# Differential attention: scores of both halves in three banks, the second softmax joined by a ratio, the division applied at the output

## What is computed

```
s = einsum("bhiqd,bhikd->bhiqk", q, k) * 64 ** -0.5      # i = 0, 1: the two half heads
p = softmax(s, axis=-1)
a = p[:, :, 0] - lam * p[:, :, 1]
o = einsum("bhqk,bhkd->bhqd", a, v)
out_da = merge_heads(rmsnorm(o, da_subln) * (1.0 - lambda_init))
```

## Time and profile before

| | us |
|---|---|
| median of 3 runs | 1944.46 (1941.73 to 1947.86) |
| the profiled execution | 1941.84 |
| its span | 1940.0 |
| PE busy in the span | 1747.5 (90%) |
| DVE busy | 756.4 (39%) |
| ACT busy | 514.0 (26%) |
| mean granted clock of PE | 0.952 |

### The profile page before, as it was taken

How to read it: one execution, slowest core, us unless ns; L and a number is a source line. 1 busy time by engine, 2 the same in 40 slices (tenths; PEclk the granted TensorE clock), 3 DMA queues, 4 the chain that set the end, 5 groups by cost and what they waited for, 6 DMA issues and landing times. The chain is left out here.

```text
span 1940.0 us, 26208 instructions
## 1 busy us (share of the span) xinstructions
PE 1747.5 (90%) x11374; PEld 1242.3 (64%) x11374; DVE 756.4 (39%) x1086; ACT 514.0 (26%) x899; POOL 138.3 (7%) x113
## 2 busy tenths in 40 slices
PE   3889999977894999999999799988895899999997
PEld 1678876656653444344443588877895478888886
DVE  2522224777434122222222577515547233333332
ACT  2311224821231110111111433233343222323231
POOL 0100000000000000000000022104411010101010
PEclk9899998988996999999999899988988999999999
DMA  9112112035323999999999523100000333322201
GB/s 365 48 44 87 44 44 87 1 139 211 128 105 123 426 430 430 430 430 429 430 429 426 215 89 113 61 1 1 5 4 1 141 141 105 111 89 87 87 1 44
DMA packets 60171, 319.19 MB, mean 165 GB/s; under 512 B 5437, under 2 KB 5773, under 8 KB 45465
## 3 DMA queue, kind: packets, MB, share of 16 engines
q1 hardware_dynamic: 60056, 317.51, 40.9%
HBM read 313.31 MB, written 4.19 MB: 164 GB/s over the span
## 5 line engine op out<-in xcount | busy, mean ns | idle before, releaser
L1508 PE MATMUL bank<-ring,xinT 128*64 128x512 f32 x592 | 131.5, 594 | 1.7 <-ACT slot_affinity L1581 1.7
L590 DVE TENSOR_TENSOR in_w_lo<-ring,in_w_hi 128x1024 fp32r<-128x1024 f32 x32 | 41.9, 1310 | 175.6 <-ACT in_w_hi L557 175.6
L250 PE MATMUL bank<-h4T_hi,mlp_w_hi 128*128 128x512 f32 (+1 forms) x288 | 105.8, 367 | 0.3 <-PEq L2460 0.3
L2635 DVE TENSOR_TENSOR mlp_w_lo<-ring,mlp_w_hi 128x1024 fp32r<-128x1024 f32 x60 | 74.0, 1234 | 80.8 <-ACT mlp_w_hi L2594 80.8
L250 PE MATMUL bank<-h4T_lo,mlp_w_hi 128*128 128x512 f32 (+1 forms) x288 | 105.2, 365 | 0.0
L250 PE MATMUL bank<-h4T_hi,mlp_w_lo 128*128 128x512 f32 (+1 forms) x288 | 105.2, 365 | 0.0
L250 PE MATMUL bank<-mlp_w_hi,up_hi 128*128 128x512 f32 x256 | 100.0, 391 | 3.5 <-DVE x L2647 3.5
L250 PE MATMUL bank<-hT_hi,in_w_hi 128*128 128x512 f32 (+1 forms) x256 | 94.6, 370 | 8.5 <-DVE hT_lo L621 4.9
L250 PE MATMUL bank<-mlp_w_hi,up_lo 128*128 128x512 f32 x256 | 99.7, 389 | 0.0
L250 PE MATMUL bank<-mlp_w_lo,up_hi 128*128 128x512 f32 x256 | 99.6, 389 | 0.0
L1508 PE MATMUL bank<-expert_slab,xinT 128*64 128x512 f32 x432 | 95.9, 594 | 0.0
(11 more groups left out here) (437 smaller groups left out, 3730.6 us busy)
## 6 DMA issues: line engine op xcount, KB each, us to landing
ring<-w_gate SPq DMA_DIRECT2D x19, 2048.0 KB, 20.9
ring<-w_up SPq DMA_DIRECT2D x18, 2048.0 KB, 20.8
ring<-w_down SPq DMA_DIRECT2D x17, 2048.0 KB, 19.7
ring<-mlp_w SPq DMA_DIRECT2D x16, 2048.0 KB, 8.5
expert_slab<-w_down SPq DMA_DIRECT2D x15, 2048.0 KB, 21.1
expert_slab<-w_up SPq DMA_DIRECT2D x14, 2048.0 KB, 19.9
expert_slab<-w_gate SPq DMA_DIRECT2D x13, 2048.0 KB, 17.3
ring<-w_ada SPq DMA_DIRECT2D x12, 2048.0 KB, 9.3
```

Of the source, the lines that this page charges most:

```text
L250: mm = pe.matmul(out, x, y, start=(start and i == 0), stop=(stop and i == 2))
L590: dve.tensor_tensor(lo, slab_part(m, s, i, by_rows), hi, ALU.subtract).then_inc(w_lo, 1)
L1508: mm = pe.matmul(bank[half * H:(half + 1) * H, b, :], xin[:, 4 * r + k, (e % 2) * H:(e % 2 + 1) * H], expert_slab(m, s)[:, k, half * COLS: ...
L2635: dve.tensor_tensor(lo, slab_part(m, s, i, n is not None), hi, ALU.subtract).then_inc(w_lo, 1)
```

## The change

- Scores of unit n lie in three banks (0 to 2 or 3 to 5, by the unit's parity), both halves side by side: 1536 columns. The matmuls have 512, 256, 512 and 256 columns, for halves 0, 1, 1, 0. Both halves touch the middle bank, so the last matmul waits on a new semaphore for the first one of half 1. One semaphore tells that both halves are there.
- Scores of unit m wait for the exps of unit m-2 and no longer for those of m-1.
- The second softmax is no longer scaled by ACT. DVE forms ratio = -lam * sum0 / sum1 and the difference is exps1 * ratio + exps0. 1/sum0 is applied as the scale of the output copy.
- Transposes go to banks 6 and 7, three blocks of 128 columns in each, and ACT copies them in two parts. The product with v goes to the columns of bank 6 that the transposes leave free; there is one such place, so product n-2 also waits for the first part of the turned difference n-1.
- The orders: PE transposes n-1, scores n+1, product n-2. DVE both reductions of n+1, then reciprocal, ratio and difference of n. ACT exp (n, first), the two copies of n-1, exp (n, second), the piece of `m.kl`, output copy n-2.
- The squares for `da_ss` move to `recurrence`, where ACT makes them from `mix_da` behind its first copy.

```diff
-            for n in range(-1, N + 2):
...
-                        if n >= 0:
-                            pe.wait_ge(exp_ready, 2 * n + 1 + i)
...
+            def turn(w):
+                pe.wait_ge(diff_ready, w + 1)
+                if w >= 2:
+                    pe.wait_ge(pv_out, w - 1)
+                for j in range(AT):
+                    mm = pe.transpose(bank[:, 6 + j // 3, (j % 3) * P:(j % 3 + 1) * P], a[:, w % 2, j * P:(j + 1) * P], m.ident)
+                    if j % 3 == 2:
+                        mm.then_inc(turned, 1)
+            def score(n):
+                h, t = units[n]
+                if n >= 2:
+                    pe.wait_ge(exp_ready, 2 * (n - 1))
+                for i, c0, c1 in ((0, 0, COLS), (1, 0, TA - COLS), (1, TA - COLS, TA), (0, COLS, TA)):
+                    r = slice(HD * i, HD * (i + 1))
+                    if (i, c0) == (0, COLS):
+                        pe.wait_ge(shared_scored, n + 1)
+                    mm = pe.matmul(scores(n, i)[:, c0:c1], q[r, h, t * P:(t + 1) * P], k[r, h, c0:c1], start=True, stop=True)
+                    if (i, c0) == (1, 0):
+                        mm.then_inc(shared_scored, 1)
+                mm.then_inc(scores_ready, 1)
+            def apply(w):
+                h = units[w][0]
+                pe.wait_ge(diffT_ready, 2 * w + 2)
+                if w + 1 < N:
+                    pe.wait_ge(diffT_ready, 2 * (w + 1) + 1)
+                else:
+                    pe.wait_ge(pv_out, w)
...
+            score(0)
+            for n in range(N + 2):
+                if 1 <= n <= N:
+                    turn(n - 1)
+                if n + 1 < N:
+                    score(n + 1)
+                if n >= 2:
+                    apply(n - 2)
...
+            for n in range(N + 2):
+                if n < N:
+                    exp_of(n, 0)
+                if 1 <= n <= N:
+                    w = n - 1
+                    for i in range(2):
+                        act.wait_ge(turned, 2 * w + i + 1)
+                        act.activation(aT[:, w % 2, i * THIRD:(i + 1) * THIRD], bank[:, 6 + i, 0:THIRD], ACT.Copy).then_inc(diffT_ready, 1)
+                if n < N:
+                    exp_of(n, 1)
...
+                    act.activation(out[:, t, h * P:(h + 1) * P], pv, ACT.Copy, scale=ri[:, w, 0:1]).then_inc(pv_out, 1)
...
+            def difference(n):
+                dve.wait_ge(exp_ready, 2 * n + 2)
+                dve.reciprocal(ri[:, n, :], rs[:, n, :]).then_inc(inv_ready, 1)
+                dve.wait_ge(inv_ready, 2 * n + 1)
+                dve.scalar_tensor_tensor(out=ratio[:, n, 0:1], in0=rs[:, n, 0:1], scalar=ri[:, n, 1:2], in1=m.neg_lam[:, :],
+                                         op0=ALU.mult, op1=ALU.mult).then_inc(inv_ready, 1)
...
+                dve.scalar_tensor_tensor(out=a[:, n % 2, :], in0=e[:, n % 2, 1, :], scalar=ratio[:, n, 0:1], in1=e[:, n % 2, 0, :],
+                                         op0=ALU.mult, op1=ALU.add).then_inc(diff_ready, 1)
+            for i in range(2):
+                bias_of(0, i)
+            for n in range(N):
+                if n + 1 < N:
+                    for i in range(2):
+                        bias_of(n + 1, i)
+                difference(n)
```

and in `recurrence`, behind ACT's first copy:

```diff
+            for t in range(TT):
+                for h in range(HEADS):
+                    n = t * HEADS + h
+                    if n:
+                        act.wait_ge(squared, n)
+                    act.activation(squares[:, :], m.mix_da[:, t, h * P:(h + 1) * P], ACT.Square, accum_out=m.da_ss[:, t, h:h + 1]).then_inc(squared, 1)
```

More of the change, by code:

```diff
@@ L650, in attention @@
     bank, q, k, v, out = m.bank, m.proj["qT"], m.proj["kT"], m.proj["v"], m.mix_da
-    HALF = TA // 2
     SCALE = HD ** -0.5
@@ L654, in attention @@
     N = len(units)
+    THIRD = AT // 2 * P
     e = m.arena("exp_scores", [P, 2, 2, TA], 92)
-    a2 = m.arena("second_softmax", [P, TA], 104)
-    a = m.arena("softmax_diff", [P, 2, TA], 107)
-    aT = m.arena("softmax_diff_T", [P, 2, TA], 113)
+    a = m.arena("softmax_diff", [P, 2, TA], 104)
+    aT = m.arena("softmax_diff_T", [P, 2, TA], 110)
     st = m.arena("softmax_stats", [P, 5, N, 2], 119)
-    mx, nb, rs, ri, rl = [st[:, i] for i in range(5)]
+    mx, nb, rs, ri, ratio = [st[:, i] for i in range(5)]
     scores_ready = m.sem("scores_ready")
+    shared_scored = m.sem("shared_scored")
     max_ready = m.sem("max_ready")
@@ L665, in attention @@
     inv_ready = m.sem("inv_ready")
-    second_ready = m.sem("second_ready")
     diff_ready = m.sem("diff_ready")
@@ L671, in attention, with scores @@
     pv_out = m.sem("pv_out")
-    squares = m.arena("da_square", [P, P], 121)
-    squared = m.sem("da_squared")
     z = (m.proj["zf"], m.proj["zb"])
+    def scores(n, i):
+        b = 3 * (n % 2)
+        return bank[:, b:b + 3, :].rearrange("p a n -> p (a n)")[:, i * TA:(i + 1) * TA]
+    pv = bank[:, 6, THIRD:THIRD + P]
     with nc.Block() as block:
@@ L683, in _ @@
         def _(pe):
-            for n in range(-1, N + 2):
-                if n + 1 < N:
-                    h, t = units[n + 1]
-                    for i in range(2):
-                        r = slice(HD * i, HD * (i + 1))
-                        if n >= 0:
-                            pe.wait_ge(exp_ready, 2 * n + 1 + i)
[L692 to L695, removed]
-                if n >= 2:
[L697 to L712, removed]
@@ new lines, in apply @@
+            def apply(w):
[5 more added lines that the diff above has]
+                    pe.wait_ge(pv_out, w)
+                for j in range(AT):
+                    mm = pe.matmul(pv, aT[:, w % 2, j * P:(j + 1) * P], v[:, j, h * P:(h + 1) * P],
+                                   start=(j == 0), stop=(j == AT - 1))
+                mm.then_inc(pv_ready, 1)
@@ L716, in exp_of @@
             def exp_of(n, i):
-                act.wait_ge(bias_ready, 2 * n + i + 1)
+                act.wait_ge(bias_ready, 2 * n + 2)
                 if n >= 2:
                     act.wait_ge(diff_ready, n - 1)
-                act.activation(e[:, n % 2, i, :].rearrange("p (a n) -> p a n", a=2), bank[:, 2 * i:2 * i + 2, 0:HALF],
-                               ACT.Exp, bias=nb[:, n, i:i + 1], scale=SCALE,
+                act.activation(e[:, n % 2, i, :], scores(n, i), ACT.Exp, bias=nb[:, n, i:i + 1], scale=SCALE,
                                accum_out=rs[:, n, i:i + 1]).then_inc(exp_ready, 1)
[L725 to L734, removed]
+            for n in range(N + 2):
[8 more added lines that the diff above has]
+                    exp_of(n, 1)
+                if n % 2 == 0 and n < N:
+                    d, h = divmod(n // 2, HEADS)
+                    act.activation(m.kl[d][:, h, :], z[d][:, h, :], ACT.Identity, bias=m.ones[:, 0:1], scale=-1.0)
                 if n >= 2:
@@ L754, in bias_of @@
             def bias_of(n, i):
-                dve.wait_ge(scores_ready, 2 * n + i + 1)
-                dve.tensor_reduce(mx[:, n, i:i + 1], bank[:, 2 * i:2 * i + 2, 0:HALF], AX.XY, ALU.max).then_inc(max_ready, 1)
+                dve.wait_ge(scores_ready, n + 1)
+                dve.tensor_reduce(mx[:, n, i:i + 1], scores(n, i), AX.X, ALU.max).then_inc(max_ready, 1)
                 dve.wait_ge(max_ready, 2 * n + i + 1)
                 dve.tensor_scalar(nb[:, n, i:i + 1], mx[:, n, i:i + 1], -SCALE, None, ALU.mult).then_inc(bias_ready, 1)
-            for n in range(-1, N):
-                if n + 1 < N:
[L762 to L777, removed]
@@ new lines, in difference @@
+            def difference(n):
[4 more added lines that the diff above has]
+                                         op0=ALU.mult, op1=ALU.mult).then_inc(inv_ready, 1)
+                dve.wait_ge(inv_ready, 2 * n + 2)
+                if n >= 2:
+                    dve.wait_ge(turned, 2 * (n - 1))
+                dve.scalar_tensor_tensor(out=a[:, n % 2, :], in0=e[:, n % 2, 1, :], scalar=ratio[:, n, 0:1], in1=e[:, n % 2, 0, :],
+                                         op0=ALU.mult, op1=ALU.add).then_inc(diff_ready, 1)
@@ L796, in recurrence @@
     rest_done = m.sem("rest_done")
+    squares = m.arena("da_square", [P, P], 121)
+    squared = m.sem("da_squared")
     bias_set, bias_in, bias_added = m.sem("ada_bias_set"), m.sem("ada_bias_in"), m.sem("ada_bias_added")
```

## The result

The changed kernel takes 1971.33 us (median of 4 runs, 1962.56 to 1972.16), the kernel before 1945.05 (1941.73 to 1947.86): ratio 1.0126, 95% interval 1.0092 to 1.0159. That is 26.3 us slower between the medians and some 24.5 us by the ratio. The forecast was slower, 1963 in 1950 to 1980.

What follows compares the result with a forecast made beforehand. No engine is full; a ring of waits in attention, two units in about 9.3 us, sets the pace. The new order adds 9.4 us plus 10.5 for low clock, 19.9 on 1941.84: 1961.7, stated 1963, range 1950 to 1980.

Steps and rivals of the forecast that it cites:

- The ring within one unit: Attention: difference n-1, transposes, scores n+1, both reductions, difference n close within one unit, 5.97 us against 4.75.
- eight terms: Attention ring: semaphore 0.05, transposes 0.75, scores 1.59, two reductions 1.06 each, reciprocal 0.19, ratio 0.25, difference 1.02 us.
- the scores until the reduction: Attention ring: time from the scores' start on PE to DVE's first reduction, costed unchanged at 1.59 us.
- stick out by 0.1: Attention scores: weight reload behind the new shared-bank wait may add 0.1 us; other bound 0.44.
- halves no longer overlap fully: Rival, attention scores: passes start in queue order, scores take 1.72 not 1.28, 6.6 us more, about 1968; chance 0.12.
- The clock: Attention: PE's idle 2.3 us per unit lets the clock fall; 5 of 14 rings low, 2.09 each, 10.5 us.
- ACT's savings are worth nothing in the new order: Attention: ACT, falling to some 3.1 us a unit, isn't in the new ring; no steady-state gain.
- Start and end: Attention at full clock: difference 0 ends at 318.66, 2.6 us early; 5.0 us follow the last difference.
- the last ring: Attention: difference 15 has no reductions before it, waits for the second exp; about 3.9 us.
- Sum of the stage: Attention: stage ends 9.4 us later at full clock, plus 10.5 for low-clock rings, total 19.9 us.
- ACT was the bound: Rival, attention: if scores run ahead, DVE's 3.6 us sets the pace, 18 us less, 1924; chance 0.06.

Runs made afterwards that it cites:

- experiment 2: The changed kernel with half 1's 256-column score matmul put first, ahead of half 0's 512 columns: 1968.97 us, ratio to before 1.0112.
- experiments 3: The changed kernel with eight idle matmuls (fillers) on PE behind each product, in its idle time: 1960.70 us, ratio to before 1.0073.
- experiment 6: The changed kernel with DVE's second reduction of unit n+1 behind the difference of n instead of ahead: 1952.32 us, ratio to before 1.0040.
- experiment 7: The changed kernel with the 16 squares back in attention, out of the next stage: 1968.16 us, ratio to before 1.0118.
- experiment 4: The kernel before with only the change's new arithmetic; banks, orders and squares as before: 1943.93 us, ratio 0.9992.
- experiment 5: The kernel before with the new arithmetic and ACT's turned-difference copy ahead of the piece for the recurrence: 1937.10 us, ratio 0.9955.

## Why the prediction was right, step by step

- **The ring within one unit** was the step that decided the sign, and it holds: DVE's wait for scores of 2.8 us in each unit, the swap that opens the ring (37 us) and cuts this wait to 0.8, the reduction moved out of it (1.06 us a unit).
- **Its size**: 6.37 for 5.97. Seven of the eight terms are as forecast within 0.06 us. The term mis-sized is the scores until the reduction, 1.93 for 1.59. I had said that the reload behind the wait may "stick out by 0.1", as half 1's 256 columns end before half 0's 512, and put it at nothing in the sum. But their signal came only after the 512 columns ahead of them in the queue; with the short matmul first it is 1.61. Over 14 rings 0.40 is 5.6 us, of which this term is 4.8 and the transposes 0.8. It is the larger part of what the forecast missed in the stage.
- **The rival "halves no longer overlap fully"** named the right place and nearly the right price (0.44), with the wrong mechanism: passes start side by side, and the signals of the ends come in order. The page "TensorE: Matmul & The Clock Gate" of the Trainium skill (Part 3: Packing small matmuls) says both start and end are in program order; experiment 2 agrees as to the end (0.32 us of a unit). As to the start, eight passes in 1.49 us do not agree.
- **The clock**: I took 5 of 14 rings at the low level, 10.5 us. From the first difference to the 15th, 97.85 us, less 14 x 6.37, leaves 8.7, and 5 rings are long here too: two at the start (8.51 and 8.15) and three of 7.9. The price of a ring at the low level was right (2.09 forecast, 2.14 in the first); those of 7.9 are only partly low. The count was luck: no row gave it, its bounds were 0 and 14, and with the short matmul first there were 7. The stage's mean clock is 0.88, where I had said around 0.8. The fillers took 7.2 us off the stage. That PE's idle time makes the falls was argued from one stretch; experiments 3 and 6 show it.
- **ACT's savings are worth nothing in the new order**: shown for the squares by experiment 7; the scaled copy was not put back in this order. For the old order I hadn't asked; experiment 4 gives zero there too, for another reason than in the new one.
- **Start and end**: the first difference ended 7.6 us after the first matmul (7.3 forecast), the last ring took 4.5 (3.9) with the clock low, the end 5.4 (5.0).
- Sum of the stage: 110.2 forecast, 115.35 found: +5.6 ring, -1.8 clock, +1.3 start, last ring and end. Another 5 us of the profiled difference lie outside the stage (1.1 before it, 4.0 behind). The forecast had nothing for them, and their cause is open; the median fell well inside the range also because the range was 30 us wide.
- **The rival "ACT was the bound"** was right in one thing: with the scores allowed to run ahead, the change does win, 12 us, but it is PE's queue that then sets the pace, at 4.55 us a unit and not at DVE's 3.6. Most of these 12 us don't need the new banks: the old order with the new arithmetic and one swap on ACT (experiment 5) was 9 us under the kernel before.

## What to carry to other kernels

With a hand-written order, follow each wait from one unit to the next and count in how many units the ring closes; a new order that closes it in one unit made the kernel some 25 us slower here, though the change removed work, and moving the scores ahead of the transposes alone gained 37. Work taken off an engine is worth what the next wait lets through, so look first for what stands behind it in the queue. And a matmul that another waits for belongs ahead of longer ones, as its signal waits for them.

## What the runs showed of the hardware

- Matmuls on the two row halves of the array run side by side, but the end of one is signalled after the end of those queued ahead of it: 256 columns queued behind 512 gave their signal late, which cost 0.3 us a unit (6.37, and 6.05 with the short one first).
- PE idle for 2.1 us in every unit of 6.4: the granted clock fell to 0.50 several times in the stage (behind the first two units, in 3 of 12 units); with fillers in that time it stayed at 1.00, and with 1.1 us idle (experiment 6) it stayed up too, after the first units. Each of the later falls cost a unit about 1.5 us (7.9 for 6.37).
- The same kernel's stage took 84.4 us in one execution and 79.8 in another, with a mean clock of 0.92 and 1.00.
- ACT's copy of 128x128 out of a bank took 0.28 us without a scale read from a tile, and 0.36 with one (kernel before, experiment 4).
